# Expert passes of a mixture-of-experts layer: TensorE's chunks as one loop over all seven groups, with tests of the loop's counter in place of groups written out before and behind it

## The reference

```python
logits = jnp.einsum('td,de->te', xf, w_router)
top_logits, top_idx = lax.top_k(logits, TOP_K)          # 2 of 8 experts per token
gates = jax.nn.softmax(top_logits, axis=-1)
...
xs = xf[tok_sorted]                                     # tokens sorted by expert
hid = jax.nn.silu(lax.ragged_dot(xs, w_gate, group_sizes)) * lax.ragged_dot(xs, w_up, group_sizes)
ys = lax.ragged_dot(hid, w_down, group_sizes)           # width 1024 -> 3584 -> 1024
ys = ys * gates.reshape(-1)[order][:, None]
out = jnp.zeros_like(xf).at[tok_sorted].add(ys)
```

## Time and profile before

| | us |
|---|---|
| runs | 5590.1, 5589.52, 5582.97 (median 5589.52) |
| profiled execution, span from first to last instruction | 5587.1 |
| PE busy in it | 5157.5 (92%) |
| expert passes in it, first to last product | 3370.5 to 5512.9 |
| PE idle in them before line 3236, released by no other engine ("issue") | 36.7 in 8 places |

### The profile page before, as it was taken

The page is one execution under the profiler, slowest core; times in us unless marked ns, Lnnn a source line. Parts: engine busy times, 40 slices in busy tenths (PEclk is TensorE's granted clock), DMA queues, the critical chain, the costliest instruction groups (busy, mean ns, idle before and its releaser), DMA issues. The chain is left out here.

```text
span 5587.1 us, 97211 instructions
## 1 busy us (share of the span) xinstructions
PE 5157.5 (92%) x38308; PEld 4523.6 (81%) x38309; DVE 2743.0 (49%) x4394; ACT 2225.6 (40%) x3437; POOL 342.1 (6%) x564
## 2 busy tenths in 40 slices
PE   7986989899899999997989988999999999999994
PEld 5675967677677899996867678989898999999994
DVE  2597545333834555554156434444444554555444
ACT  2454236333443444443234423333334444444432
POOL 0111100000600000000023001000000000000001
PEclk8997999999999999998999999999999999999997
DMA  2110010310003655553100425444444555555444
GB/s 88 35 66 17 0 37 1 134 51 30 8 12 123 244 209 205 191 208 115 46 16 19 139 113 185 155 157 158 164 158 175 184 195 186 194 196 188 181 157 188
DMA packets 104610, 688.52 MB, mean 123 GB/s; under 512 B 12320, under 2 KB 16304, under 8 KB 63280
## 3 DMA queue, kind: packets, MB, share of 16 engines
q1 hardware_dynamic: 90752, 639.74, 31.6%
q0 software_dynamic: 8816, 27.44, 1.3%
q10 hardware_dynamic: 4800, 17.83, 0.8%
HBM read 622.67 MB, written 62.29 MB: 123 GB/s over the span
## 5 line engine op out<-in xcount | busy, mean ns | idle before, releaser
L3374 DVE TENSOR_TENSOR experts_low<-experts_raw,experts_high 128x1024 fp32r<-128x1024 f32 x678 | 810.5, 1223 | 982.9 <-ACT experts_high L3301 982.9
L3236 PE MATMUL ps<-experts_xs_high,experts_high 128*128 128x256 f32 (+1 forms) x3584 | 1036.1, 289 | 39.0 <-issue 36.7
L3236 PE MATMUL ps<-experts_xs_low,experts_high 128*128 128x256 f32 (+1 forms) x3584 | 1034.3, 289 | 0.0
L3236 PE MATMUL ps<-experts_xs_high,experts_low 128*128 128x256 f32 (+1 forms) x3584 | 1034.3, 289 | 0.0
L3236 PEld LDWEIGHTS ps<-experts_xs_high,experts_high 128*128 128x128 f32 x3584 | 679.3, 190 | 50.5 <-issue 42.4
L3301 ACT ACTIVATE experts_high<-experts_raw 128x1024 fp32r<-128x1024 f32 x678 | 687.8, 1050 | 40.9 <-DMA experts_raw<-experts 40.9
L3236 PEld LDWEIGHTS ps<-experts_xs_low,experts_high 128*128 128x128 f32 x3584 | 679.4, 190 | 8.1
L3236 PEld LDWEIGHTS ps<-experts_xs_high,experts_low 128*128 128x128 f32 x3584 | 679.1, 189 | 0.4 <-issue 0.4
L2913 PE MATMUL ps<-dense_xs_parts,dense_high 128*128 128x256 f32 x2816 | 499.6, 280 | 7.0 <-DVE dense_low L3022 5.9
L2913 PEld LDWEIGHTS ps<-dense_xs_parts,dense_high 128*128 128x128 f32 x2816 | 437.0, 189 | 14.2 <-issue 7.8
L3228 PE MATMUL ps<-experts_high,experts_hid_high 128*128 128x512 f32 x1120 | 438.5, 392 | 0.0
(11 more groups left out here) (538 smaller groups left out, 9096.3 us busy)
## 6 DMA issues: line engine op xcount, KB each, us to landing
experts_raw<-experts SPq DMA_DIRECT2D x226, 1536.0 KB, 6.4
dense_raw<-dense SPq DMA_DIRECT2D x90, 1536.0 KB, 6.3
mixT<-w_in SPq DMA_DIRECT2D x36, 512.0 KB, 3.3
y_slot<-mla_blank SPq DMA_DIRECT2D x15, 1152.0 KB, 21.1
out_proj_raw<-w_out SPq DMA_DIRECT2D x48, 256.0 KB, 2.8
proj_keys_raw<-w_in SPq DMA_DIRECT2D x20, 512.0 KB, 3.2
x_mixed<-mixT SPq DMA_DIRECT2D x16, 512.0 KB, 2.6
h_rows<-out_proj_rows SPq DMA_DIRECT2D x16, 512.0 KB, 2.6
```

The costliest lines, as they stand in the source:

```text
L3236: last = nc.tensor.matmul(ps[:, m, 0:width], w[:, u, m, c], x[:, k, 0:width], start=(k == 0 and i == 0), stop=(k == KD - 1 and i == 2))
L3374: nc.vector.tensor_tensor(low[:, v, t, :], raw[:, v % NR, t, :], high[:, v, t, :].bitcast(F32), ALU.subtract).then_inc(split, 1)
```

## The change

On PE the expert passes no longer use `chunks`. One loop runs over all seven groups of four chunks, in each of the two bodies. What the first and the last chunk do differently stands under tests of the group counter inside the loop: chunk 0 of the group does its down products only where `g > 0`; chunk 1 has two copies of them, one for `g > 0` and one for the first group, with the two waits; chunk 3 has one for all but the last group and one with the transposes and the pass's end. The multiplications that are executed, their order and their waits are the same. The other engines keep `chunks`, and their instructions do not change.

```diff
-                def one(f, u):
-                    n = j * NC + f
+                def one(g, u):
+                    n = j * NC + g * NB + u
...
                     product(1, u).then_inc(up_made, 1)
-                    if isinstance(f, int) and f == 0:
-                        return
-                    if isinstance(f, int) and f == 1:
-
-                        pe.wait_ge(y_main, j + 1)
-                        pe.wait_ge(y_rest, j + 1)
-                    pe.wait_ge(hid_split, n)
-                    pe.wait_ge(split, 3 * n + SPLIT0)
-                    core.settle(pe)
                     v = (u - 1) % NB
-                    if not (isinstance(f, int) and f == NC - 1):
+
+                    def down_before(first):
+
+                        pe.wait_ge(hid_split, n)
+                        pe.wait_ge(split, 3 * n + SPLIT0)
+                        core.settle(pe)
                         for a in range(n_tiles):
-                            last = down_tile(v, a, isinstance(f, int) and f == 1, False)
+                            last = down_tile(v, a, first, False)
                         last.then_inc(down, 1)
-                        return
...
+                    if u == 0:
+                        with pe.If(g > 0):
+                            down_before(False)
+                    elif u == 1:
+                        with pe.If(g > 0):
+                            down_before(False)
+                        with pe.Else():
+
+                            pe.wait_ge(y_main, j + 1)
+                            pe.wait_ge(y_rest, j + 1)
+                            down_before(True)
+                    elif u < NB - 1:
+                        down_before(False)
+                    else:
+                        with pe.If(g < NC // NB - 1):
+                            down_before(False)
+                        with pe.Else():
+                            down_before_and_turn()
+                with pe.Fori(0, NC // NB, 1) as g:
+                    for u in range(NB):
+                        one(g, u)
```

## The result

The changed kernel takes 5559.17 us (median of 4 runs, 5557.36 to 5563.51) beside 5587.88 us (4 runs) for the kernel before: a ratio of 0.9946 on record, 95% interval 0.9932 to 0.9960 (the two medians alone give 0.9949). That is 28.7 us less, 4.4 us under the forecast of 5563.6 and inside its range. The profiled execution has a span of 5554.7 us, 32.4 us less than that of before.

A forecast was written before the change was run, and what follows sets the result against it. PE was taken as the bound, idle 30.0 us at six pass boundaries where far jumps fetch code. Boundary gains of 25.9 us, branches at nothing, took 5589.5 to 5563.6 us; own range 5553 to 5570, eight-in-ten range 5552 to 5581.

The forecast's parts named there:

- The code stays: PE between passes: some 730 instructions come round, under the 993 believed to stay, so far jumps find their code present.
- The exception at the first boundary: First wide-to-wide boundary: code not yet fetched; 2.2 us idle, 12.8 products, 1.65 slow clock, given as 16.8 us.
- ACT's chain is late next: Pass starts: ACT's sum copy, table load and SiLU then delay PE; 13.4 us narrow to narrow, 14.9 to 15.3 elsewhere.
- the 1 to 2.5 that I named: Sign of being right: a pass's second gate product waits 1 to 2.5 us idle until ACT's SiLU releases it.
- The openings: Boundary idle time plus four products, up to a pass's first down product; forecast 13.4 to 16.8 us each.
- Branches at nothing: PE's 168 tests, 96 taken jumps and 16 more back edges hide under queued products and cost nothing.
- The sum: Gains at the six pass boundaries that had idle time, together 25.9 us, between bounds of 16.0 and 42.6.
- Code leaving at boundaries: Rival: PE's code still leaves its store between passes, both far jumps stay, time as before, 5589 us; chance 0.12.
- a loop that does not stay: Rival: each of 48 back edges in the pass loops stalls 3.1 us, 149 us slower, 5739 us; chance 0.03.
- branches that show: Rival: PE's taken jumps cost time, 0.22 us each eating the gain, 0.5 us giving 5624 us; chance 0.08.
- The lower clock: Rival: PE's waits on ACT at boundaries lower its clock, 1.65 us six times; gain 16.0, 5573.5 us; chance 0.17.
- the 993 instructions of the RWKV loop: Evidence: RWKV chunk loop of 993 PE instructions came round without code packets, so passes of 1,600 were judged too long.

The follow-up runs named there:

- Experiment 1: Changed kernel with the last group of four chunks written out again behind the loop, first group still folded in: 5561.99 us, ratio 0.9947.
- experiments 2: Changed kernel plus 20 never-executed gate products (960 PE instructions) behind chunk 2's down products in each loop, under an always-skipping test: 5570.92 us, ratio 0.9962.
- Experiments 8 and 9: Changed kernel with POOL, not ACT, storing the sums: 5550.36 us; the same with DVE also multiplying SiLU and up product before splitting weights: 5554.49 us.
- Experiment 3: Changed kernel with two more PE tests in each chunk, 448 in all, each choosing between identical branches: 5558.74 us, ratio 0.9942.
- Experiment 4: The changed kernel run again without edits, beside other variants on one chip: 5564.68 us, ratio 0.9953.
- experiment 10: The changed kernel run again without edits, beside the two kernels with stores on POOL: 5561.30 us, ratio 0.9941.

## Why the prediction was right

- *The code stays.* Five of six boundaries have no idle time by "issue" before the first gate product, and a narrow pass fetches no code. Experiment 1 shows that a pass of 1,230 instructions stays too, where one of 1,590 did not. The Trainium skill ("Runtime: NRT & Kernel Launch", section "Instruction fetch mechanics") would have had the loops stall at jumps out of a two-page window; the trace disagrees for PE, with loops of 710 instructions and passes of 1,230 that come round without a packet.
- *The exception at the first boundary.* It is there, with 1.89 us of idle time against 2.2 forecast. The term was 1.3 us too large all the same: I added 1.65 for a slow clock, and the clock stayed at 1.00; and 2.2, 12.8 and 1.65 make 16.65, not 16.8. This is the term that was mis-sized most. That the clock stayed is not a rule: in experiments 2, 8 and 9 it fell behind this boundary, and the four products took 14.39, 14.40 and 14.40 us.
- *ACT's chain is late next.* At the second wide-to-wide and the three narrow-to-narrow boundaries ACT's SiLU releases the second gate product after 1.25 to 1.66 us of idle time, at the wide-to-narrow one after 2.92, longer than the 1 to 2.5 that I named. The openings are within 0.3 us of the forecast elsewhere. Experiments 8 and 9 show the cause, not only the fit: without the stores on ACT the waits are gone.
- *Branches at nothing.* Experiment 3 shows it.
- *The sum.* 26.3 us against 25.9. Of the median's 4.4 us below the forecast, 1.6 are the kernel before, whose median moved from 5589.52 to 5587.88 with a fourth run, 0.4 are the openings, and the rest is the scatter outside them.
- *The rivals.* Code leaving at boundaries, a loop that does not stay, and branches that show all fell. The lower clock did not decide either, but it does happen, at one boundary: in experiments 1, 3 and 4 it fell behind the wide-to-narrow boundary's wait for ACT. Experiment 4 is the changed kernel itself; that opening took 15.53 us there instead of 15.20 (see the last section).

One reading of the prediction was wrong: the 993 instructions of the RWKV loop. The number fits a count that takes each of the loop's 448 products once, with a weight load, and 97 other instructions. The trace of the kernel before has every product twice: one round has 896 products, 896 weight loads and the 97, some 1,890. That these are what is fetched shows ahead of the loop, from 505.6 to 548.3 us, where 8 code packets come for 1,998 products and weight loads, one for some 250. The kernel before, one round and the stretch ahead of the loop (PE, then PEld), and the code packets of that stretch:

```profile
583.71:613.72 30.01, 29.37 (x896) 28.92 (x896) 16.79 (x46) 8.59 (x30) 3.68 (x6) 1.00 0.00 0
...
505.60:548.30 42.70, 36.94 (x1001) 35.31 (x997) 18.40 (x48) 9.70 (x33) 3.68 (x6) 0.96 0.01 3
...
q8 instruction: 8, 0.13, 1.3%
```

So a loop of some 1,890 instructions came round without a packet in the same kernel in which a pass of 1,590 did not. Length alone is not the rule, and that a pass of 1,600 is too long for PE's store does not follow. What sets a pass apart from that loop is its jump over the other body; whether the jump, or code fetched beyond it, pushes a part out is open (experiment 2). The forecast needed only that some 730 instructions stay, and they are fewer than either count.

## What to carry to other kernels

When an engine stops at a loop's edge and no semaphore ends the wait, look for code packets at that time, and look at all that lies on the way round, jumped-over code too; written-out first and last groups can cost more in fetched code than they save in tests. Where such a stop goes, ask which other engine had been hidden behind it, and take its work out of the chain: that was worth another 11 us. Before a wait goes into an in-order queue, list what stands behind it there; on SP it cost 65 us against the changed kernel beside it, on an idle POOL nothing within the passes and some 5 us behind them.

## What the runs showed of the hardware that I had not expected

The length of an idle time alone does not set the granted clock. In the changed kernel PE stood 2.92 us before 4243.64 and kept 1.00. In the kernel of experiment 3 it stood 2.03 us before 4242.91, and the next stretch was at 0.51, half speed:

```profile
4243.40:4246.80 3.40, 3.40 (x18) 3.40 (x18) 2.69 (x3) 1.59 (x4) 0.00 (x0) 0.51 0.93 378
```

That opening took 15.02 us, no longer than the 15.20 of the changed kernel. The same kernel can do either: in experiment 4 the changed kernel stood 2.63 us before 4242.59 and went on at half speed; in experiment 10 it stood 2.59 at this place and kept 1.00. The stretch of experiment 4:

```profile
4242.40:4245.70 3.30, 3.11 (x14) 3.15 (x15) 2.28 (x3) 1.93 (x3) 0.00 (x0) 0.50 0.97 396
```

With the stores on POOL, 2.46 us before the first wide-to-wide boundary's gate product were followed by 3.4 us at 0.50, and that opening, which has no other wait, is 1.6 us longer than its like (14.40 beside 12.80). What else decides, no run here separates.
